# Two transformer blocks on one core: the wait for a stored table moved later, loads and norms at both ends reordered, queries computed over 258 columns

## The chip, the core and the metric

The kernel runs on one core of a Trainium2 chip. The metric is the device time of one execution, in microseconds (us). The engines have these names in profiles: PE is TensorE (matmuls; PEld its weight loads), DVE is VectorE, ACT is ScalarE, POOL is GpSimd, and SP is SyncE, which here only issues DMAs. A q behind a name (SPq) is the engine's own instruction queue.

## The reference, cut to what matters

A sequence of 256 tokens with 16 learned meta tokens ahead of it (L = 272 positions, D = 2048 features) goes through a first block; the 256 real tokens then go through a second one. All is float32.

```python
h = concat([meta, x])                                  # 272 positions
proj = rmsnorm(h, mix_norm_g) @ w_in                   # q, k, v of 8 + latents cq (512), ckv (256), k_pe (64)
out_a = neighbourhood_attention(q_a, k_a, v_a, rpb, meta_bias)   # 8 heads of 128, 4 x 64 grid
out_b = mla_attention(cq, ckv, k_pe, ...)              # 8 heads; q = rmsnorm(cq) @ w_q_up, k and v from ckv
h = h + concat([rmsnorm(out_a), rmsnorm(out_b)]) @ w_out
h = h + conv_glu(rmsnorm(h), ...)                      # width-3 convolution over positions
h = h[:, 16:]
# second block
proj = rms_norm(h, norm_mix) @ w_in_2
ya = moba_attention(q, k, v, rel_table)                # softmax(q k / sqrt(d) + rel_table[bucket(distance)])
yb = multiscale_pool(u, ...); yc = stick_breaking_attention(...)
h = h + (gates * branches(ya, yb, yc)) @ w_out_2
h = h + swiglu(rms_norm(h, norm_ffn))
out = rms_norm(h, norm_final)
```

## The kernel before, in words

Everything is stored transposed: features on the 128 partitions, positions along the free axis. `h` is 16 blocks of 128 x 272. A float32 product is made of three matmuls in a rounded type (fp32r): each operand is split in a high part and the rest (`xh`, `xl` for activations, `whi`, `wlo` for weights), and PE adds hi x hi, hi x lo and lo x hi (lines 1166 to 1168).

**The weight stream.** All weights come as 930 or so chunks of 128 x 1024 (512 KB), in the order of use, into four buffers `raw` (SP, line 307). ACT rounds a chunk (`high_part`, `whi`, line 414), DVE subtracts (`low_part`, `wlo`, line 718), and PE uses it. Both run two chunks ahead of PE (`AHEAD`). A new load goes out when DVE has made the low half of the buffer's chunk. A chunk is 24 matmuls of 128x128 weights (four output blocks `ob`, two contraction tiles, three products). A group is a run of chunks that fills the four banks of `acc`, which DVE empties. Every engine's program is written out in a fixed order; what another engine must have done is waited for by counting semaphores.

**The start.** SP issues the gains (`vec`), then in turn chunk and quarter of `h` (lines 310 to 313). ACT rounds chunks 0 and 1, then for each quarter of `h`: four `xh` blocks, the squares of the quarter, two chunks. DVE: low parts of chunks 0 and 1, then for each quarter four `xl` blocks, adding the squares into `ss`, `x_ready`, two low parts. PE starts on a pair of chunks when `x_ready` has counted a quarter. The norm's factor is applied when `acc` is emptied (`times_rms`).

**The first block's stages.** CQ (8 chunks) makes the query latent, CKV (8) the key latent, QUP (6) the queries of the latent attention (MLA), KVUP (4) its keys and values. Then QKV: 6 groups of 8 chunks make q, k, v of the neighbourhood attention (NA), 4 heads at a time, and between the chunks the eight MLA heads are computed, six chunks to a head (steps 0 to 5), NA heads 0 to 3 beside MLA heads 4 to 7. The other NA heads run beside the OUTB groups.

**The stored distances.** For the second block's attention a table of 8 heads x 512 distances is made just before QKV (PE line 1256, DVE line 905), in `dist`, which lies in the buffer `quad_a`. POOL writes it to DRAM 128 times over by one DMA of 2 MB (line 337), whose outermost dimension is the 8 heads. `quad_a` is also where NA's scores go (`sx_na`). DVE waits for the stored copy (`dist_stored`) ahead of the whole QKV loop. On POOL's queue the NA mask and the NA bias follow behind that DMA (lines 341 to 361); NA's first scores (step 2 of MLA head 4) need the bias.

**The end.** The last projection (DOWN2, 4 groups of 22 chunks) adds to `h`; after each group ACT squares four blocks (line 438) and DVE adds them to `ss`. Then one matmul with ones sums over partitions (line 1183), ACT takes Ln and Exp (lines 423, 425), DVE multiplies each of the 16 blocks by gain and factor (line 1142), and SP stores four quarters (line 324).

## Time and profile before

| | |
|---|---|
| median of 3 runs | 2908.0 us (2906.98 to 2910.27) |
| profiled execution | 2907.43 us, of which the span of its instructions 2905.7 us |
| PE busy | 2810.6 us, 97% of the span |
| DVE busy | 1654.5 us, 57% |
| ACT busy | 1244.4 us, 43% |
| POOL busy | 114.9 us, 4% |
| DMA | 499.99 MB, mean 172 GB/s |
| chain that ended last | PE 91%; DVE 3%; ACT 2%; DMA 2% |

PE's busy time counts modelled ends of pipelined matmuls; the distance between the starts of matmuls is the better measure of what one costs. The chain that ended last is followed back from the last instruction to what released each step; a share in it is time that shortening would give back, as long as nothing else is just behind. All times within the execution count from the start of its span.

### The profile page before, as it was taken

The page shows a single profiled execution, that of the slowest core. Times are in us where ns is not written, and L with a number is a line of the kernel's source. Part 1 is how long each engine was busy: PE and PEld are TensorE (multiplying, and loading weights), DVE is VectorE, ACT ScalarE, POOL GpSimd, SP SyncE. Part 2 cuts the span into 40 slices and gives each one's busy share as a digit, 9 for nine tenths or more (in the row PEclk, how much of TensorE's full clock was granted, in tenths as well). Part 3 has the DMA queues.
Part 4 walks back from the last instruction along what each step waited for, and adds up shares of the span by engine and source line. Part 5 has one row for each costly group of instructions (what it writes and reads, how often), then busy time and mean ns, then how long its engine had stood idle before and what let it go on. Part 6 is the DMA issues. An engine that isn't in the chain of part 4 may idle for free.

```text
span 2905.7 us, 58853 instructions
## 1 busy us (share of the span) xinstructions
PE 2810.6 (97%) x22990; PEld 2767.5 (95%) x22990; DVE 1654.5 (57%) x2128; ACT 1244.4 (43%) x1512; POOL 114.9 (4%) x133
## 2 busy tenths in 40 slices
PE   7589999999999999999999999999999999999997
PEld 7578899999999999999999999999999999999997
DVE  6255678666666654455555766555655555555444
ACT  5135555344343443443444555444443444334333
POOL 0001230000000000000000500000000000000000
PEclk9799999999999999999999999999999999999999
DMA  6433354555555554555555445555555555555545
GB/s 207 92 118 113 109 133 147 192 189 176 193 173 188 186 189 170 184 183 180 181 175 175 153 166 182 182 183 177 188 181 182 175 195 187 186 181 188 188 161 174
DMA packets 141133, 499.99 MB, mean 172 GB/s; under 512 B 17405, under 2 KB 19837, under 8 KB 141024
## 3 DMA queue, kind: packets, MB, share of 16 engines
q1 hardware_dynamic: 136912, 491.36, 49.8%
q0 software_dynamic: 4112, 7.02, 1.7%
q8 instruction: 87, 1.43, 0.2%
q14 instruction: 22, 0.18, 0.0%
HBM read 494.06 MB, written 4.19 MB: 171 GB/s over the span
## 4 chain that ended last, share of the span: by engine, by line
PE 91%; DVE 3%; ACT 2%; DMA 2%; issue 1%; DVEq 1%; ACTq 0%; SPq 0%
PE acc L1166 29%; PE acc L1168 28%; PE acc L1167 28%; DMA distances<-quads 2%; DVE wlo L718 1%; PE aux L1208 1%; ACT whi L414 1%; PE aux L1199 1%; PE aux L1271 0%; PE aux L1273 0%; PE aux L1265 0%; ACT quads L438 0%; DVE h L760 0%; DVE ss L745 0%; PE aux L1383 0%
## 5 line engine op out<-in xcount | busy, mean ns | idle before, releaser
L718 DVE TENSOR_TENSOR wlo<-raw,whi 128x1024 fp32r<-128x1024 f32 x926 | 1121.7, 1230 | 894.6 <-ACT whi L414 844.8
L1166 PE MATMUL acc<-xh,whi 128*128 128x256 f32 (+2 forms) x4976 | 1418.3, 285 | 63.3 <-DVE wlo L718 44.5
L1168 PE MATMUL acc<-xh,wlo 128*128 128x256 f32 (+2 forms) x4976 | 1404.4, 282 | 0.0
L1167 PE MATMUL acc<-xl,whi 128*128 128x256 f32 (+2 forms) x4976 | 1401.6, 282 | 0.0
L414 ACT ACTIVATE whi<-raw 128x1024 fp32r<-128x1024 f32 x926 | 954.5, 1054 | 858.1 <-PE acc L1168 813.3
L1166 PEld LDWEIGHTS acc<-xh,whi 128*128 128x128 f32 x4976 | 941.0, 189 | 74.2 <-DVE wlo L718 47.7
L1167 PEld LDWEIGHTS acc<-xl,whi 128*128 128x128 f32 x4976 | 938.6, 189 | 0.7
L1168 PEld LDWEIGHTS acc<-xh,wlo 128*128 128x128 f32 x4976 | 938.5, 189 | 0.0
L1166 PE MATMUL acc<-acth,whi 128*128 128x256 f32 x1408 | 398.0, 283 | 6.3 <-issue 6.3
L1167 PE MATMUL acc<-actl,whi 128*128 128x256 f32 x1408 | 397.5, 282 | 0.0
L1168 PE MATMUL acc<-acth,wlo 128*128 128x256 f32 x1408 | 397.3, 282 | 0.0
L1166 PEld LDWEIGHTS acc<-acth,whi 128*128 128x128 f32 x1408 | 267.3, 190 | 7.0 <-issue 6.7
L1167 PEld LDWEIGHTS acc<-actl,whi 128*128 128x128 f32 x1408 | 267.4, 190 | 0.0
L1168 PEld LDWEIGHTS acc<-acth,wlo 128*128 128x128 f32 x1408 | 267.3, 190 | 0.0
L738 DVE TENSOR_TENSOR quads<-acc,rstd 128x256 f32<-128x256 f32 (+2 forms) x140 | 59.0, 425 | 66.1 <-PE acc L1168 63.9
L1166 PE MATMUL acc<-mh,whi 128*128 128x256 f32 x256 | 72.3, 283 | 0.0
L1167 PE MATMUL acc<-ml,whi 128*128 128x256 f32 x256 | 71.9, 281 | 0.0
L1168 PE MATMUL acc<-mh,wlo 128*128 128x256 f32 x256 | 71.9, 281 | 0.0
L611 ACT ACTIVATE acth<-quads 128x1024 f32 (+1 forms) x22 | 23.3, 1060 | 113.0 <-DVE quads L1025 113.0
L608 ACT ACTIVATE quads<-quads 128x1024 f32<-128x1024 f32 x22 | 23.3, 1060 | 108.8 <-DVE quads L1011 56.3
L370 POOL DMA_DIRECT2D bias<-distances x16 | 8.7, 541 | 1113.0 <-PE acc L1168 829.6
L1025 DVE TENSOR_TENSOR quads<-acc,quads 128x256 f32<-128x256 f32 x88 | 37.4, 424 | 20.3 <-PE acc L1168 20.2
(272 smaller groups left out, 2360.8 us busy)
## 6 DMA issues: line engine op xcount, KB each, us to landing
raw<-in_wts SPq DMA_DIRECT2D x928, 512.0 KB, 4.2
h<-in_hT SPq DMA_DIRECT2D x4, 544.0 KB, 8.4
distances<-quads POOLq DMA_DIRECT2D x1, 2048.0 KB, 44.9
bias<-distances POOLq DMA_DIRECT2D x16, 128.0 KB, 2.4
out_T<-h SPq DMA_DIRECT2D x4, 512.0 KB, 2.9
bias<-in_rp POOLq DMA_DIRECT2D x16, 64.0 KB, 4.8
bias<-in_rp POOLq DMA_DIRECT2D x8, 44.0 KB, 4.4
bias<-in_rp POOLq DMA_DIRECT2D x8, 42.0 KB, 4.3
```

Source lines behind the costliest of these rows:

```text
L370: pool.dma_start(bias2[:, t, :], bass.AP(dist_dram.tensor, i * (DISTS + 1) + (SEQ - 1 - t * P), [[HEADS * (DISTS + 1) - 1, P], [1, SEQ]])) ...
L414: act.activation(whi[:, slot_of(at, j), :], raw[:, slot_of(at, j), :], ACT.Copy).then_inc(hi_ready, 1)
L608: act.activation(quad_b[:, :, 0:SEQ], quad_b[:, :, 0:SEQ], ACT.Silu).then_inc(silu_out, 1)
L611: act.activation(acth[:, bass.ds(i * 4, 4), :], quad_a[:, :, 0:SEQ], ACT.Copy).then_inc(act_hi, 1)
L718: dve.tensor_tensor(wlo[:, slot_of(at, j), :], raw[:, slot_of(at, j), :], whi[:, slot_of(at, j), :].bitcast(F32), ALU.subtract).then_inc(l ...
L738: dve.tensor_tensor(dst(ob), acc[0:rows, ob, 0:n], scale[0:rows, cols], ALU.mult)\
L1025: dve.tensor_tensor(quad_a[:, ob, 0:SEQ], acc[:, ob, 0:SEQ], quad_b[:, ob, 0:SEQ], ALU.mult)\
L1166: pe.matmul(dst, hi, x_hi(kt), start=kt == 0, stop=False)
L1167: pe.matmul(dst, hi, x_lo(kt), start=False, stop=False)
L1168: last = pe.matmul(dst, lo, x_hi(kt), start=False, stop=kt == chunks * per_chunk - 1)
L1199: last = pe.transpose(aux[0:nk, kt, t * a.rows:(t + 1) * a.rows], a.sx[0:a.rows, t, k:k + nk], ident_s[0:a.rows, 0:a.rows])
L1208: last = pe.matmul(aux[:, 3, 0:a.nq], a.vt[0:nk, kt, :], a.pt[0:nk, kt, 0:a.nq], start=kt == 0, stop=kt == len(a.kt) - 1)
```

## The change

Four things are done.

1. DVE's wait for `dist_stored` moves from ahead of the QKV loop to just ahead of the first NA scores (step 2, `na == 0`).
2. Queries are computed only for the 258 positions from `Q0` = 14 on (`xtail`): in CQ, in the two QUP groups and the two rope groups, and in the q groups of QKV. The unused 14 columns of `qnope`, `qrope` and the q part of `qkv` are set to zero at the start.
3. At the start SP issues the first quarter of `h` ahead of the first chunk, and waits for quarter 0 before it issues chunk 1 and for quarter 1 before it issues quarter 2. ACT and DVE do the first quarter of `xh` and `xl` before the first two chunks. `x_ready` now counts every two blocks of `xl`, before the squares, and PE waits for it chunk by chunk; the squares have a count of their own (`sq_used`). Later waits on `x_ready` are shifted by 4.
4. At the end the final gain is multiplied into `h` by ACT (`times_final_g`), block by block after the squares of each of the first three groups and after Exp for the last; the last four blocks are squared one by one and summed over partitions by PE, without DVE's additions; DVE multiplies a whole quarter by the factor in one instruction. ACT's and DVE's loops over the groups of DOWN2 are written out.

```diff
             sp.dma_start(vec[:], vecs).then_inc(vec_landed, 16)
-            for q in range(4):
-                load(q, q)
+            def load_h(q):
                 sp.dma_start(h[:, 4 * q:4 * q + 4, :], hT[:, 4 * q:4 * q + 4, :]).then_inc(h_landed[q], 16)
+
+            load_h(0)
+            load(0, 0)
+            sp.wait_ge(h_landed[0], 16)
+            load(1, 1)
+            load_h(1)
+            load(2, 2)
+            sp.wait_ge(h_landed[1], 16)
+            load_h(2)
+            load(3, 3)
+            load_h(3)
...
-            high_parts(At(-AHEAD, 0), AHEAD)
             for q in range(4):
                 act.wait_ge(h_landed[q], 16)
-                if q:
-                    act.wait_ge(x_ready, q)
                 for b in range(4 * q, 4 * q + 4):
                     act.activation(xh[:, b, :], h[:, b, :], ACT.Copy, scale=vec[:, VEC["mix_g"] + b:VEC["mix_g"] + b + 1])\
                         .then_inc(xh_ready, 1)
+                if q == 0:
+                    high_part(At(-AHEAD, 0), 0)
+                    high_part(At(-AHEAD, 0), 1)
+                else:
+                    act.wait_ge(sq_used, q)
                 act.activation(quad_b[:, :, :], h[:, 4 * q:4 * q + 4, :], ACT.Square).then_inc(sq_ready, 1)
...
+            def times_final_g(b):
+                act.activation(h[:, b, META:L], h[:, b, META:L], ACT.Copy,
+                               scale=vec[:, VEC["final_g"] + b:VEC["final_g"] + b + 1]).then_inc(hg_ready, 1)
+
+            for k in range(3):
+                residual(AT_DOWN2.past(k * CF, k), 4 * k, None, slice(META, L), None, CF)
+                act.drain()
+                for b in range(4 * k, 4 * k + 4):
+                    times_final_g(b)
+            at = AT_DOWN2.past(3 * CF, 3)
+            high_parts(at, CF)
+            act.wait_ge(x_ready, 23)
+            for ob in range(4):
+                act.wait_ge(bank_free, groups_behind(at, 4, 4 + ob + 1))
+                act.activation(quad_b[:, ob, 0:SEQ], h[:, DB - 4 + ob, META:L], ACT.Square).then_inc(sq_ready, 1)
+            inv_rms(rstd[:, META:L], aux[:, 3, META:L], D, ss_sum, 7, rs_ready)
+            for b in range(DB - 4, DB):
+                times_final_g(b)
...
-            low_parts(At(-AHEAD, 0), AHEAD)
             dve.wait_ge(vec_landed, 16)
             for q in range(4):
...
+                    if b % 2:
+                        last.then_inc(x_ready, 1)
+                if q == 0:
+                    low_part(At(-AHEAD, 0), 0)
+                    low_part(At(-AHEAD, 0), 1)
                 dve.wait_ge(sq_ready, q + 1)
-                add_squares(L).then_inc(x_ready, 1)
+                add_squares(L).then_inc(sq_used, 1)
...
             dve.memset(ss_na[:], 0.0)
-            dve.wait_ge(dist_stored, 16)
             for j in range(6 * CD):
...
                 elif step == 2:
+                    if na == 0:
+                        dve.wait_ge(dist_stored, 16)
                     if na >= 0:
                         scaled_scores(NA, na, bias, (bias_masked, na + 1))
...
             dve.wait_ge(rs_ready, 7)
-            for b in range(DB):
-                last = dve.scalar_tensor_tensor(h[:, b, META:L], h[:, b, META:L],
-                                                vec[:, VEC["final_g"] + b:VEC["final_g"] + b + 1], rstd[:, META:L],
-                                                ALU.mult, ALU.mult)
-                if b % 4 == 3:
-                    last.then_inc(out_ready, 1)
+            for q in range(4):
+                dve.wait_ge(hg_ready, 4 * q + 4)
+                hq = h[:, 4 * q:4 * q + 4, META:L]
+                dve.tensor_tensor(hq, hq, rstd[:, META:L].unsqueeze(1).to_broadcast([P, 4, SEQ]), ALU.mult)\
+                    .then_inc(out_ready, 1)
...
             for j in range(CD):
-                if j % 2 == 0:
-                    pe.wait_ge(x_ready, j // 2 + 1)
-                chunk(AT_CQ, j, CD, x1(xh), x1(xl), L)
+                pe.wait_ge(x_ready, j + 1)
+                chunk(AT_CQ, j, CD, xtail(xh), xtail(xl), NQ)
...
-            group(AT_QUP, 2, x1(lath), x1(latl), L)
+            group(AT_QUP, 2, xtail(lath), xtail(latl), NQ)
...
             for j in range(6 * CD):
-                chunk(AT_QKV.past(j // CD * CD, j // CD), j % CD, CD, x1(xh), x1(xl), L)
+                if j // CD % 3 == 0:
+                    chunk(AT_QKV.past(j // CD * CD, j // CD), j % CD, CD, xtail(xh), xtail(xl), NQ)
+                else:
+                    chunk(AT_QKV.past(j // CD * CD, j // CD), j % CD, CD, x1(xh), x1(xl), L)
...
-            token_sums(x_ready, 20)
+            pe.wait_ge(x_ready, 23)
+            pe.matmul(aux[:, 3, META:L], ones_s[:], ss[:, META:L], start=True, stop=False)
+            for ob in range(4):
+                pe.wait_ge(sq_ready, 20 + ob)
+                last = pe.matmul(aux[:, 3, META:L], ones_s[:], quad_b[:, ob, 0:SEQ], start=False, stop=ob == 3)
+            last.then_inc(ss_sum, 1)
```

DVE's order where the QKV loop begins, before: `wlo` is the low part of a weight chunk, `rs_a` is cleared to hold NA's sums, `aux` holds MLA head 0's rotated queries.

```order
L905 TENSOR_TENSOR quads<-aux,neg_s 8x512 [waits dist_sum]
L907 MEMSET rs_a 128x272
L718 TENSOR_TENSOR wlo<-raw,whi 128x1024 [waits hi_ready,dist_stored]
L816 TENSOR_TENSOR sqr<-aux,tab 64x272 [waits mla_sums]
L817 TENSOR_TENSOR qg<-qg,tab 64x272
L718 TENSOR_TENSOR wlo<-raw,whi 128x1024 [waits hi_ready]
```

The same place and the place of the first NA scores, in the changed kernel (about 100 DVE instructions lie between the two):

```order
L939 TENSOR_TENSOR quads<-aux,neg_s 8x512 [waits dist_sum]
L941 MEMSET rs_a 128x272
L744 TENSOR_TENSOR wlo<-raw,whi 128x1024 [waits hi_ready]
L842 TENSOR_TENSOR sqr<-aux,tab 64x272 [waits mla_sums]
...
L855 TENSOR_TENSOR kr<-tab,sq_60 64x272
L857 TENSOR_TENSOR qr<-sqr,sq_60 64x258
L812 SCALAR_TENSOR_TENSOR quads<-aux,bias 86x816 [waits bias_masked,na_scores,dist_stored]
L815 TENSOR_REDUCE quads<-quads 86x3
```

The wait has left the low part of a chunk and now stands on the instruction that already waits for the NA bias.

SP's order at the start, as the difference between the two programs (+ is the changed kernel; `raw` is a weight chunk):

```order
 L310 DMA vec<-in_vecs 128x292
+L312 DMA h<-in_hT 128x1088
 L307 DMA raw<-in_wts 128x1024
-L313 DMA h<-in_hT 128x1088
+L307 DMA raw<-in_wts 128x1024 [waits h_landed0]
+L312 DMA h<-in_hT 128x1088
 L307 DMA raw<-in_wts 128x1024
-L313 DMA h<-in_hT 128x1088
+L312 DMA h<-in_hT 128x1088 [waits h_landed1]
 L307 DMA raw<-in_wts 128x1024
```

Quarter 0 of `h` now goes first, and chunk 1 and quarter 2 each wait for a landed quarter.

DVE's order at the end, before and then in the changed kernel (`h<-acc,h` empties the last group; `ss` holds the summed squares):

```order
L745 TENSOR_TENSOR ss<-ss,quads 128x256 [waits sq_ready]
L745 TENSOR_TENSOR ss<-ss,quads 128x256 x3
L1136 REGISTER_ALU
L1136 COMPARE_AND_BRANCH
L1142 SCALAR_TENSOR_TENSOR h<-h,vec,rstd 128x256 [waits rs_ready]
L1142 SCALAR_TENSOR_TENSOR h<-h,vec,rstd 128x256 x15
```

```order
L744 TENSOR_TENSOR wlo<-raw,whi 128x1024 [waits hi_ready] x22
L786 TENSOR_TENSOR h<-acc,h 128x256 [waits block_done] x3
L786 TENSOR_TENSOR h<-acc,h 128x256 [waits chunk_used]
L1178 TENSOR_TENSOR h<-h,rstd 128x4x256 [waits hg_ready,rs_ready]
L1178 TENSOR_TENSOR h<-h,rstd 128x4x256 [waits hg_ready] x3
```

The four additions of squares are gone from behind the last group, and sixteen instructions have become four.

## Rows read from the trace of the kernel before

**Rows 1.** The page: the chain that ended last, by line.

```profile
PE acc L1166 29%; PE acc L1168 28%; PE acc L1167 28%; DMA distances<-quads 2%; DVE wlo L718 1%; PE aux L1208 1%; ACT whi L414 1%; PE aux L1199 1%; PE aux L1271 0%; PE aux L1273 0%; PE aux L1265 0%; ACT quads L438 0%; DVE h L760 0%; DVE ss L745 0%; PE aux L1383 0%
```

**Rows 2.** Waits, 105 to 152 us: who for whom, total, times, longest us.

```profile
DVE wlo L718 <- DMA distances<-quads: 45.0, 1, 45.0
```

**Rows 3.** Windows: us, busy PE, PEld, DVE, ACT, POOL; PEclk; DMA share; GB/s.

```profile
113.40:151.20 37.80, 0.00 (x0) 0.00 (x0) 1.19 (x2) 1.53 (x2) 0.00 (x0) 0.53 0.46 51
151.30:156.80 5.50, 5.50 (x24) 5.50 (x25) 4.92 (x9) 0.00 (x0) 4.92 (x7) 0.50 0.76 204
```

**Rows 4.** Timeline of PE: start us, us, line, out<-in [idle before <-releaser].

```profile
107.07 1.08 PE L1262 MATMUL aux<-sq,ones_s 128*128 128x272 f32 x4
...
110.35 0.29 PE L1167 MATMUL acc<-xl,whi 128*128 128x272 f32 x1
...
113.10 0.29 PE L1168 MATMUL acc<-xh,wlo 128*128 128x272 f32 x1
151.29 0.59 PE L1166 MATMUL acc<-xh,whi 128*128 128x272 f32 x1 [37.89 <-DVE wlo L718]
...
156.86 1.31 PE L1271 MATMUL aux<-kn,qn 128*86 128x272 f32 x5
...
202.25 0.85 PE L1262 MATMUL aux<-sq,ones_s 128*128 128x272 f32 x3
...
211.70 1.15 PE L1271 MATMUL aux<-kn,qn 128*86 128x272 f32 x4
```

**Rows 5.** DMA queues, 112 to 150 us: packets, MB, share of 16 engines.

```profile
q0 software_dynamic: 477, 1.97, 47.6%
```

**Rows 6.** The page: the weight queue over the whole span, in the same columns.

```profile
q1 hardware_dynamic: 136912, 491.36, 49.8%
```

**Rows 7.** DMA issues, 203 to 204 us: one weight load, KB, us to landing.

```profile
raw<-in_wts SPq DMA_DIRECT2D x1, 512.0 KB, 3.3
```

**Rows 8.** Timeline of ACT, 199 to 218 us.

```profile
200.79 1.05 ACT L414 ACTIVATE whi<-raw 128x1024 fp32r<-128x1024 f32 x1
...
217.57 1.05 ACT L414 ACTIVATE whi<-raw 128x1024 fp32r<-128x1024 f32 x1
```

**Rows 9.** Timeline of POOL and DVE: the first bias masked, the first NA scores.

```profile
160.75 1.94 POOL L361 TENSOR_TENSOR bias<-bias,mask_s 86x816 f32<-86x816 f32 x1 [3.95 <-DMA bias<-in_rp]
...
265.97 0.99 DVE L786 SCALAR_TENSOR_TENSOR quads<-aux,bias 86x816 f32<-86x816 f32 x1
```

**Rows 10.** DMA issues, one at 1.32 us and one at 1.79 us.

```profile
raw<-in_wts SPq DMA_DIRECT2D x1, 512.0 KB, 4.0
...
h<-in_hT SPq DMA_DIRECT2D x1, 544.0 KB, 5.3
```

**Rows 11.** Timeline of ACT, DVE and PE at the start.

```profile
9.94 1.74 ACT L498 ACTIVATE xh<-h,vec 128x272 fp32r<-128x272 f32 x4
...
12.86 2.00 DVE L745 TENSOR_TENSOR ss<-ss,quads 128x272 f32<-128x272 f32 x4
...
14.91 0.60 PE L1166 MATMUL acc<-xh,whi 128*128 128x272 f32 x1 [14.91 <-DVE ss L745]
```

**Rows 12.** Timeline of ACT, 545 to 575 us (chunks of 258 columns; five steps).

```profile
557.13 1.06 ACT L414 ACTIVATE whi<-raw 128x1024 fp32r<-128x1024 f32 x1 [1.83 <-PE acc L1168]
...
571.56 1.06 ACT L414 ACTIVATE whi<-raw 128x1024 fp32r<-128x1024 f32 x1 [1.82 <-PE acc L1168]
```

**Rows 13.** Timeline of PE and DVE at the end.

```profile
2893.96 0.98 PE L1183 MATMUL aux<-ss,ones_s 128*128 128x272 f32 x2 [3.81 <-DVE ss L745]
...
2896.00 6.42 DVE L1142 SCALAR_TENSOR_TENSOR h<-h,vec,rstd 128x256 f32<-128x256 f32 x16 [2.09 <-ACT rstd L425]
```

**Rows 14.** Groups by line and form, DVE: busy us, mean ns | idle before.

```profile
L1020 DVE TENSOR_TENSOR quads<-quads,rstd 128x1024 f32<-128x1024 f32 x11 | 13.4, 1218 | 0.0
```

**Rows 15.** DMA queues, 2896 to 2906 us.

```profile
q1 hardware_dynamic: 2112, 2.10, 61.3%
```

**Rows 16.** Timeline of DVE between the first two DOWN2 groups.

```profile
2702.38 4.62 DVE L718 TENSOR_TENSOR wlo<-raw,whi 128x1024 fp32r<-128x1024 f32 x4
```

More of the change, by code:

```diff
@@ L232, in build @@
         xh_ready = sem("xh_ready")
-        sq_ready = sem("sq_ready")
+        sq_ready, sq_used = sem("sq_ready"), sem("sq_used")
         x_ready = sem("x_ready")
@@ L503, in _, with latent @@
             inv_rms(rstd[:], aux[:, 3, 0:L], D, ss_sum, 1, rs_ready)
-            def latent(at, k0, blocks, gain):
+            def latent(at, k0, blocks, gain, c0):
                 act.wait_ge(bank_free, groups_behind(at, 4, 4 + 4))
                 for k in range(blocks):
-                    act.activation(lath[:, k0 + k, :], quad_a[:, k, :], ACT.Copy, scale=vec[:, gain + k:gain + k + 1])
-                return act.activation(quad_b[:, 0:blocks, :], quad_a[:, 0:blocks, :], ACT.Square)
-            latent(AT_CQ, 0, CQB, VEC["cq_g"]).then_inc(lat_hi, 1)
+                    act.activation(lath[:, k0 + k, c0:L], quad_a[:, k, c0:L], ACT.Copy,
+                                   scale=vec[:, gain + k:gain + k + 1])
+                return act.activation(quad_b[:, 0:blocks, c0:L], quad_a[:, 0:blocks, c0:L], ACT.Square)
+            latent(AT_CQ, 0, CQB, VEC["cq_g"], Q0).then_inc(lat_hi, 1)
             high_parts(AT_CKV, 4)
-            inv_rms(rs_a[:], aux[:, 3, 0:L], CQB * P, lat_sum, 1, lat_rs)
+            inv_rms(rs_a[:, Q0:L], aux[:, 3, Q0:L], CQB * P, lat_sum, 1, lat_rs)
             for j in range(4, CD):
                 high_part(AT_CKV, j)
-            latent(AT_CKV, CQB, CKVB, VEC["ckv_g"])
+            latent(AT_CKV, CQB, CKVB, VEC["ckv_g"], 0)
             act.activation(kpe_g, kpe, ACT.Copy, scale=vec[0:ROPE, VEC["k_rope_g"]:VEC["k_rope_g"] + 1])
@@ L705, in _ @@
             act.preload_act_table_set(LN_EXP)
-            with act.Fori(0, 2) as i:
-                for k in range(2):
-                    residual(shifted(Turn(AT_DOWN2, i, 2 * CF, 2), k * CF, k), i * 8 + 4 * k, None, slice(META, L), None,
-                             CF)
-            inv_rms(rstd[:], aux[:, 3, 0:L], D, ss_sum, 7, rs_ready)
+            def times_final_g(b):
[15 more added lines that the diff above has]
+                times_final_g(b)
         @block.vector
@@ L843, in _ @@
             dve.memset(ss[:], 0.0)
+            for q in (qnope[:, :, 0:Q0], qrope[:, :, 0:Q0], qkv[:, 0:HEADS, 0:Q0]):
+                dve.memset(q, 0.0)
             dve.drain()
@@ L915, in evict_group @@
                         half, part = divmod(j // CD, 3)
+                        c0 = 0 if part else Q0
                         times_rms(AT_QKV.past(j - CD + 1, j // CD), CD,
-                                  lambda ob: qkv[:, part * HEADS + 4 * half + ob, :], slice(0, L))
+                                  lambda ob: qkv[:, part * HEADS + 4 * half + ob, c0:L], slice(c0, L))
                 if step == 0:
@@ L1238, in _ @@
                     for k in range(CQB):
-                        last = pe.matmul(aux[:, 3, 0:L], ones_s[:], quad_b[:, k, :], start=k == 0, stop=k == CQB - 1)
+                        last = pe.matmul(aux[:, 3, Q0:L], ones_s[:], quad_b[:, k, Q0:L], start=k == 0, stop=k == CQB - 1)
                     last.then_inc(lat_sum, 1)
             pe.wait_ge(lat_ready, 1)
-            group(AT_QUP, 2, x1(lath), x1(latl), L)
-            group(AT_QUP.past(2, 1), 2, x1(lath), x1(latl), L)
+            group(AT_QUP, 2, xtail(lath), xtail(latl), NQ)
+            group(AT_QUP.past(2, 1), 2, xtail(lath), xtail(latl), NQ)
             for g in range(2):
-                group(AT_QUP.past(4 + g, 2 + g), 1, x1(lath), x1(latl), L, width=ROPE, row=4 * ROPE, per_chunk=4)
+                group(AT_QUP.past(4 + g, 2 + g), 1, xtail(lath), xtail(latl), NQ, width=ROPE, row=4 * ROPE, per_chunk=4)
             pe.wait_ge(lat_hi, 2)
```

34 lines of the change are left out of this document (18 added, 16 removed).

## The prediction

> **What bounds the kernel now.** I read the chain that ended last first. It is PE almost throughout: the three product lines make 85% of it [rows 1]. So a change pays if it takes columns from PE or idle time from in front of it. One entry is not an engine: the store of the distances is 2% of the chain, some 45 us. The waits of the stretch from 105 to 152 us show where it sits: DVE's low part of a weight chunk waits 45.0 us for that DMA [rows 2], and behind this instruction PE stands idle 37.89 us [rows 4]. The windows show the rest: PE's clock is at its lower level of 1.2 GHz for the 5.50 us that follow the idle time (PEclk 0.50) [rows 3]. At the ends the trace shows two more stretches in which PE is not at work: PE starts at 14.91 us [rows 11], and behind the last product come 3.81 us of idle time, one matmul and a tail from 2896.00 us on [rows 13].
>
> **Part 1, the wait.** What it costs is read from PE's timeline, by the same piece of program with and without it. In MLA head 0 the square sums start at 107.07 us and the first scores at 156.86, 49.8 us later; in head 2, which like head 0 has no group to empty there, it is 202.25 to 211.70, 9.45 us [rows 4]. The difference, 40.3 us, holds the idle time and the slow clock behind it. What is late next at that place is what is late in head 2, so it is in the 9.45 already. The wait itself lands on DVE's first NA scores. Behind them on DVE stand all the low parts of weights, and PE would wait for these; but before the change the first NA scores come at 265.97 us [rows 9], and the transfer had landed at 150 (105 + 45.0). Moved up by 40, they still come some 75 us after it. The bias stands behind the transfer on POOL's queue: it was masked at 162.7 us [rows 9], and nothing of that moves as long as the transfer takes its 45 us, which leaves over 60 us too (265.97 - 40.3 - 162.7).
>
> What is new is that weight loads now run beside the transfer; the trace has no such stretch. The transfer alone keeps 47.6% of 16 DMA engines busy at 477 packets in 38 us [rows 5]. If it is spread over all 16, the loads have 52% left and need about 35% in this stage, and nothing is lost. If it sits on the 8 engines of its outermost dimension, these are 95% busy, with 60 packets each in 38 us, 0.64 us a packet. A weight row of 4 KB costs 2905.7 x 16 x 0.498 / 136912 = 0.17 us of an engine [rows 6]. A load is 8 such rows per engine; taken in turn with the transfer's packets it takes 8 x (0.64 + 0.17) = 6.5 us, where the stage uses a load every (202.25 - 107.07 - 40.3) / 12 = 4.6 us [rows 4]. So each falls back 1.9 us, some 13 us over the 7 loads that fit in 45 us. Against it stands slack: a load goes out when the low half behind the high part of 200.79 us is made, at 203.2, lands 3.3 us later [rows 7] and is used at 217.57 [rows 8], 11 us to spare; and PE itself is two chunks behind ACT. What could leak through are scores and exponentials that ACT does behind a late chunk. Ends: 0 and 8 us; I take 1.5, near the free end, because the spare 11 us swallows most of 13. Part 1: -40.3 + 1.5.
>
> The Trainium skill ("DMA: Bandwidth & Descriptors", Rules for kernel authors) says that an access pattern whose slowest dimension is below 16 confines a DMA to at most that many engines, here 8. That speaks for the second case; 47.6% of 16 fits 8 busy engines, though it doesn't prove it.
>
> **Part 2, 258 columns.** From 110.35 to 113.10 us lie 22 starts of 272-column matmuls: 125 ns each [rows 4]. Chunks of 258 columns follow at (571.56 - 557.13) / 5 = 2.886 us, 120.2 ns a matmul [rows 12]. So 5 ns each. Affected are 8 chunks of 24 in CQ (192), 96 + 96 in QUP, 384 in QKV's q groups. QUP and QKV: 576 x 5 = 2.9 us; CQ is in part 3. Ends: 1.5, if the waits on DVE in each head eat the half, and 3.2. DVE's and ACT's shorter instructions between CQ and CKV, about a dozen on the path, give 14 columns or some 15 ns each: 0.2 us. The three small memsets are before any data has landed.
>
> A rule of the skill ("TensorE: Matmul & The Clock Gate", Back-to-back issue gap) has the spacing set by weight load and matmul together. Were the weight load alone the limit, 14 columns would buy nothing; the two spacings above differ, so the trace is against that.
>
> **Part 3, the start.** Loads land almost in the order of issue: the first at 1.32 + 4.0 = 5.3 us, the second at 1.79 + 5.3 = 7.1 [rows 10]. Now the quarter of h is first, so it is there at about 5.4, the chunk at 7.1. ACT: `xh` 5.5 to 7.2 (1.74 for four [rows 11]), high part 0 (1.05 [rows 8]) to 8.25. DVE: `xl` to 7.9, low part 0 (1.2, the last of 4.62 us for four [rows 16]) to 9.5. PE starts at 9.5 where it started at 14.91: 5.4 us. SP's new waits set what comes next: chunk 1 goes out at 5.5 and lands at 8.7, quarter 1 at 10.1, chunk 2 at 11.5, chunk 3 only after quarter 1, at 14.7. ACT does high part 3 ahead of the second quarter: to 15.8, then `xh`; DVE low part 3 to 17.0, two `xl` blocks to 17.9. PE, on its slow clock first (24 took 5.50 us with 272 columns [rows 3], so some 5.2), ends chunk 0 at 14.7, chunk 1 at 17.6, and waits 0.3. From there each pair of chunks takes PE 5.8 us and DVE 1.65 + 1.9 (squares, from 2.00 [rows 11]) + 2.3 = 5.8, a tie. `x_ready` no longer waits for the squares, which is why PE can run at all at this pace. At CQ's end the gain is then 5.4, plus 192 x 5 ns = 1.0, less 0.3 and 0.1: 6.0 us. Ends: 3, if chunk 3 or the clock's rise is 3 us later, and 7.
>
> **Part 4, the end.** The last product ends at 2893.96 - 3.81 = 2890.15 us. Emptying the bank takes to 2890.7, one Square block 0.44 (a quarter of 1.74 [rows 11]) to 2891.2, one matmul of half of 0.98 [rows 13], since the other sums are already in the bank, to 2891.7; Ln and Exp take as now 2896.00 - 2894.94 = 1.06, to 2892.8. DVE starts 3.2 us earlier. Its four instructions take 1.22 us each [rows 14] against 6.42 for sixteen [rows 13]; ACT's last four gains (1.74) end before the fourth. The stores are then the limit: their packets take 61.3% of 10 us, 6.1 us on 16 engines [rows 15], close to the 6.42. So of the 1.5 us that DVE saves, only the earlier first store (1.3 instead of 1.6) and the closed gaps (0.3 to 0.6) count: 0.8. Part 4: 4.0 us; ends 3.0 and 4.7.
>
> In the three earlier groups ACT has the four gains (1.74, with a drain 1.8) between the squares and the next high part, the one for the group's chunk 2. PE wants that chunk two chunks after the last product, 5.7 us. Before: emptying 0.6, squares 1.05, DVE's additions 2.0 [rows 11], low part 1.2 [rows 16]: 4.9. Now ACT's side is the longer one: 0.6 + 1.05 + 1.8 + 1.05 (high part) + 1.2 = 5.7, and waits between engines of 0.2 make 5.9. PE stands 0.2 us, at two of the boundaries: 0.4; ends 0 and 0.8.
>
> **Sum.** -40.3 + 1.5 - 2.9 - 0.2 - 6.0 - 4.0 + 0.4 = -51.5 us. The profiled execution took 2907.4, so 2855.9; the median of the runs is 0.6 higher: 2856.5 us.
>
> **The rivals.**
> - Weights late beside the transfer. For it: 95% busy engines, if they are 8. Against: 11 us of slack. Full price 8 instead of 1.5: 2863. The skill's rule on engines (above) makes this the rival it names. Chance 0.13.
> - The start gives back its gain: SP, blocked on quarter 0 and 1, leaves the DMA engines idle, chunk 3 and then `xl` come 3 us later: 2859.5. For it: two round trips of about 5 us are now in series. Against: the stores of work ACT and DVE have meanwhile. Chance 0.10.
> - Columns buy nothing (the skill's weight-load rule): 2.9 and 1.0 lost, 2860.4. The measured spacings are against it: 0.02.
> - The change doesn't do what it says: the 45 us come back at the first NA scores or the bias. It would need the transfer to last 60 us longer; then the wait is the excess. 0.01.
> - Slower than before. The mechanism: on the shared engines the transfer goes first, and the loads land only when it ends. PE still has the four chunks whose weights were in at 105 us, four times 4.6 us from 113 on, so it stands from about 131. With the transfer's 45 us this costs 19 us and 3 for the slow clock, 2877, still faster. To be slower by 0.2%, 2913.8, PE must lose 57 us there, which asks for a transfer of 26 + 57 = 83 us, 1.85 times the one seen, with no load landing. For it: nobody has seen the two together. Against: queues of equal kinds shared the engines at the start, where every load landed. Chance 0.02, with 0.02 more for the 2877.
>
> **How the numbers follow.** The forecast has 0.70. Within it: start 3 to 7, columns 1.5 to 3.2, end 3.0 to 4.7, contention 0 to 4, and one period of slow clock more or fewer elsewhere, worth half of 5.5 us [rows 3]. Few of these go wrong together: 2850 to 2862. The range takes in the first two rivals and most of their sum: 2849 to 2866. What a measurement can tell from no change is 0.2%, 5.8 us. Only the slower rival and the return of the wait reach that side: faster 0.97, same 0.01, slower 0.02.
>
> **What would show it.** PE's idle time at 113 us gone, the clock at full level from about 15 us to the first DOWN group; the distances' time to landing between 45 and 60 us and the weight loads beside it at 3 to 8 us instead of 3.3; no wait on `dist_stored` in the list. First matmul at 9 to 10 us, CQ's end 6 us earlier. Chunks of q groups at 2.89 us. DVE's last stretch four instructions of 1.2 us, beginning some 3 us earlier behind the last product, and the span ending 11.5 us behind it instead of 15.6. The prediction is wrong if the raw loads land later than 14 us beside the transfer, if ACT waits for them there, or if PE waits for `xl` in CQ by more than 1 us in total.

## The result, and the profile after

The changed kernel takes 2871.6 us (median of 4 runs, 2868.3 to 2875.0), the kernel before beside it 2907.5 (2906.8 to 2910.3). The ratio is 0.9875, with a 95% interval of 0.9858 to 0.9892. The change gains 36 us, not 51, and ends 5.6 us above the range forecast. The profiled execution took 2870.8 us with a span of 2869.1.

The page's chain of the changed kernel, by line, answers [rows 1]; the row of the weight queue, q1, answers [rows 6]. In the rows below q0 is GpSimd's software queue and q10 ScalarE's hardware queue.

```profile
q1 hardware_dynamic: 136912, 491.36, 52.4%
...
PE acc L1199 29%; PE acc L1201 29%; PE acc L1200 29%; DVE wlo L744 1%; DMA raw<-in_wts 1%; ACT whi L424 1%; PE aux L1241 1%; PE aux L1232 0%; PE aux L1306 0%; PE aux L1308 0%; DMA h<-in_hT 0%; PE aux L1300 0%; DVE h L786 0%; PE aux L1421 0%
```

The store of the distances is gone from the chain, and 1% of `raw<-in_wts` is new: weight loads. The waits between 90 and 180 us (who for whom, total, times, longest) say how much, where [rows 2] had the one wait of 45.0.

```profile
POOL bias L358 <- issue: 47.7, 1, 47.7
DVE wlo L744 <- ACT whi L424: 30.1, 10, 8.3
ACT whi L424 <- DMA raw<-in_wts: 23.5, 6, 8.4
```

VectorE no longer waits for the store. (The first row is POOL's own: the neighbourhood attention's mask goes out just behind the store, at 101.74 us, and lands with it, 48.1 us later. The first bias is masked at 161.9 us and used at 234.3, so nobody waits for it.) ScalarE waits 23.5 us for weights, and VectorE's low parts wait behind it. The DMA issues at 97.4, 104.5, 113.2 and 117.7 us (KB, us to landing), and the store's own, answer [rows 7].

```profile
raw<-in_wts SPq DMA_DIRECT2D x1, 512.0 KB, 3.3
...
raw<-in_wts SPq DMA_DIRECT2D x1, 512.0 KB, 21.8
...
raw<-in_wts SPq DMA_DIRECT2D x1, 512.0 KB, 25.7
...
raw<-in_wts SPq DMA_DIRECT2D x1, 512.0 KB, 27.4
...
distances<-quads POOLq DMA_DIRECT2D x1, 2048.0 KB, 47.8
```

A load takes 3.3 us alone and up to 27.4 us beside the store. (A further load, issued at 109.9 us, takes 22.7.) ScalarE's timeline shows the rhythm in which they arrive, where [rows 8] had no wait.

```profile
126.39 1.06 ACT L424 ACTIVATE whi<-raw 128x1024 fp32r<-128x1024 f32 x1 [8.44 <-DMA raw<-in_wts]
132.64 1.06 ACT L424 ACTIVATE whi<-raw 128x1024 fp32r<-128x1024 f32 x1 [4.71 <-DMA raw<-in_wts]
138.90 1.06 ACT L424 ACTIVATE whi<-raw 128x1024 fp32r<-128x1024 f32 x1 [2.88 <-DMA raw<-in_wts]
145.18 1.06 ACT L424 ACTIVATE whi<-raw 128x1024 fp32r<-128x1024 f32 x1 [3.46 <-DMA raw<-in_wts]
```

The starts are 6.26 us apart: that is the 6.5 us for a load that takes turns with the store. New is the 8.44 us in front of the first. PE's longest waits here are one of 5.40 us, which ends at 147.98, and this one:

```profile
129.19 2.59 PE L1241 MATMUL aux<-pt,vt 91*128 91x258 f32 x6 [4.47 <-DVE pt L830]
```

In the windows (columns as in [rows 3]) the second and third are stretches at the lower clock; one begins right behind PE's wait, the other 1.4 us before its end.

```profile
100.00:148.00 48.00, 36.68 (x245) 31.61 (x243) 17.62 (x30) 17.63 (x35) 2.47 (x3) 0.95 0.61 117
129.50:132.90 3.40, 3.40 (x13) 2.94 (x12) 0.00 (x0) 0.26 (x1) 0.00 (x0) 0.50 0.78 165
146.60:153.40 6.80, 5.42 (x24) 5.45 (x25) 5.47 (x11) 2.12 (x2) 2.57 (x3) 0.50 0.51 193
```

The start and the end, from the timelines of PE, ScalarE and VectorE, answer [rows 11] and [rows 13].

```profile
10.22 0.55 PE L1199 MATMUL acc<-xh,whi 128*128 128x258 f32 x1 [10.22 <-DVE wlo L744]
...
19.51 0.39 PE L1199 MATMUL acc<-xh,whi 128*128 128x258 f32 x1 [1.84 <-DVE xl L881]
...
16.31 1.06 ACT L424 ACTIVATE whi<-raw 128x1024 fp32r<-128x1024 f32 x1 [2.77 <-DMA raw<-in_wts]
17.28 1.75 ACT L505 ACTIVATE xh<-h,vec 128x272 fp32r<-128x272 f32 x4
...
2856.64 0.28 PE L1201 MATMUL acc<-acth,wlo 128*128 128x256 f32 x1
2856.76 0.59 PE L1490 MATMUL aux<-ss,ones_s 128*128 128x256 f32 x2
2857.19 1.89 PE L1493 MATMUL aux<-quads,ones_s 128*128 128x256 f32 x8
...
2860.11 4.63 DVE L1178 TENSOR_TENSOR h<-h,rstd 128x1024 f32<-128x1024 f32 x4 [2.72 <-ACT rstd L435]
```

PE starts 4.7 us earlier, at 10.22 (4.2 us against the second trace of before, see experiment 1); the wait of 2.77 us for chunk 3 then makes `xh` late, and PE stands 1.84 us from 17.7 on. From the start of the last product to the span's end it is now 12.45 us, against 15.86 in the first trace of before and 16.15 in the second. All three signs by which the prediction called itself wrong are there: loads later than 14 us, ScalarE's waits for them, and PE's wait for `xl` of over 1 us.

### The profile page after: what moved, and what is told of

Same layout as the page of the kernel before. It is cut to its first block, busy times and chain, and to the rows that moved or that the text cites. A ratio compares the mean times of both kernels' runs of the same rounds, so it can differ in the third digit from the quotient of the medians.

```text
span 2869.1 us, 58709 instructions
## 1 busy us (share of the span) xinstructions
PE 2811.4 (98%) x22998; PEld 2767.3 (96%) x22998; DVE 1651.9 (58%) x2115; ACT 1251.6 (44%) x1531; POOL 114.2 (4%) x133
## 4 chain that ended last, share of the span: by engine, by line
PE 91%; DVE 3%; ACT 2%; DMA 1%; issue 1%; DVEq 1%; ACTq 0%; SPq 0%
PE acc L1199 29%; PE acc L1201 29%; PE acc L1200 29%; DVE wlo L744 1%; DMA raw<-in_wts 1%; ACT whi L424 1%; PE aux L1241 1%; PE aux L1232 0%; PE aux L1306 0%; PE aux L1308 0%; DMA h<-in_hT 0%; PE aux L1300 0%; DVE h L786 0%; PE aux L1421 0%; PE aux L1314 0%
## 5 line engine op out<-in xcount | busy, mean ns | idle before, releaser
L1199 PE MATMUL acc<-xh,whi 128*128 128x256 f32 (+2 forms) x4976 | 1419.1, 285 | 26.4 <-DVE wlo L744 16.7
L764 DVE TENSOR_TENSOR quads<-acc,rstd 128x256 f32<-128x256 f32 (+1 forms) x140 | 59.0, 425 | 65.1 <-PE acc L1201 64.3
## 6 DMA issues: line engine op xcount, KB each, us to landing
distances<-quads POOLq DMA_DIRECT2D x1, 2048.0 KB, 47.8
```

What stands on the lines that cost most here:

```text
L764: dve.tensor_tensor(dst(ob), acc[0:rows, ob, 0:n], scale[0:rows, cols], ALU.mult)\
L1199: pe.matmul(dst, hi, x_hi(kt), start=kt == 0, stop=False)
```

## The experiments

All ratios are against the kernel before, run beside them. The changed kernel itself was timed only with the result; differences from it are differences of medians from other rounds, in which the kernel before had medians of 2907.1 to 2908.8 us. So such a difference under some 2 us says nothing. "Lead" is how much earlier than in the kernel before VectorE makes the low part of the same weight chunk.

**1. The kernel before, once more.** Nothing is edited; it serves as a second trace. The expectation counts the traces read until then.

> The kernel before once more, unchanged, for a second trace of it on another chip. All eight traces of other kernels so far show the turn of 16 chunks in the second feed-forward network at 45.58 us, the one trace of the kernel before at 45.37 us, 2.1 us over its eleven turns. If the kernel sets it, this trace has 45.37 again. If the chip or the execution does, it has 45.58, and 2 us of the leads read against the old trace are no effect of the change.

Windows of the second feed-forward network in the first trace of before, the second, and the changed kernel:

```profile
2200.00:2600.00 400.00, 400.00 (x3386) 400.00 (x3385) 220.58 (x231) 162.65 (x160) 0.00 (x0) 1.00 0.54 184
```

```profile
2200.00:2600.00 400.00, 400.00 (x3371) 400.00 (x3370) 219.75 (x230) 162.46 (x159) 0.00 (x0) 1.00 0.55 183
```

```profile
2200.00:2600.00 400.00, 400.00 (x3371) 400.00 (x3369) 216.46 (x226) 160.70 (x157) 0.00 (x0) 1.00 0.56 186
```

In the same 400 us the first trace has 3386 matmuls, the other two 3371. From one turn of 16 chunks to the next it is 45.60 us in VectorE's low parts here, as in all traces but the first, which has 45.39 (the expectation has 45.58 and 45.37; the 0.21 between them is the same). So the kernel does not set it; the execution or the chip does. The second trace (2906.1 us, span 2904.5) also lacks the slow clock of the first at 1133 to 1140 us, so leads against the old trace were off by up to 4.6 us. All leads in the table below are read against the second.

**2. Only the wait moved**, in the kernel before. The line taken out stands ahead of the QKV loop, the new ones in step 2 of each head:

```diff
-            dve.wait_ge(dist_stored, 16)
...
+                    if na == 0:
+                        dve.wait_ge(dist_stored, 16)
```

> The kernel before with only VectorE's wait for the stored distances moved to the first neighbourhood scores; order of the loads, the norms at both ends and the columns as before. Theory A: the wait gives back only 25 to 27 us of its 40.3, as in the changed kernel: 2880 to 2883 us, and PE waits in the stage for late loads. Theory B1 (the stall comes from the earlier start, which puts loads and store in another phase): the wait gives its 39 to 40 us, 2867 to 2869 us. The turn of 16 chunks in the second feed-forward network takes 45.39 us as in the kernel before if PE's code position sets it (PE's instructions are those of before), 45.60 us if the other engines' do.

2881.9 us (2881.0 to 2883.0), ratio 0.9912 (0.9895 to 0.9928): 25.5 us gained. The load issued at 109.8 us and the one at 123.1, and ScalarE's waits for weights from 90 to 270 us:

```profile
raw<-in_wts SPq DMA_DIRECT2D x1, 512.0 KB, 21.8
...
raw<-in_wts SPq DMA_DIRECT2D x1, 512.0 KB, 27.4
```

```profile
ACT whi L414 <- DMA raw<-in_wts: 23.5, 6, 8.3
```

These are the changed kernel's numbers, so neither the new start nor the columns have a part in them: theory A holds, B1 falls.

**3. The store in 16 gated pieces**, in the changed kernel. The run without the store that the expectation names gave no time. Its theory B: VectorE and ScalarE hold the stage back by their order or by the clock, and the store only coincides. The two waits for the store count to 256 here.

```diff
-            pool.dma_start(dist_dram.rearrange("c h d -> h c d"), dist.unsqueeze(1).to_broadcast([HEADS, P, DISTS + 1]))\
-                .then_inc(dist_stored, 16)
+            for n in range(16):
+                pool.wait_ge(chunk_used, AT_QKV.n + n)
+                pool.dma_start(dist_dram[8 * n:8 * n + 8].rearrange("c h d -> h c d"),
+                               dist.unsqueeze(1).to_broadcast([HEADS, 8, DISTS + 1])).then_inc(dist_stored, 16)
```

> The changed kernel with the store issued as 16 DMAs of 8 copies, the n-th once PE has used n chunks of the QKV products. Same bytes, spread over some 45 us. Theory A (a load waits behind what the store has queued ahead of it on the shared engines): a piece holds those engines for 3 us, a load lands after at most 3.3 + 3 = 6.3 us where the ring of four chunks allows about 11 us, so nothing waits and the time is that of the kernel without the store, 2857 to 2860 us. Theory A' (the shared rate alone counts, however the store is cut): loads land after 16 to 27 us as now, 2869 to 2874 us. Theory B as for the run without the store: no change.

2857.3 us (2855.3 to 2859.1), ratio 0.9829 (0.9812 to 0.9845), 14.3 us below the changed kernel. The first load beside a piece (103.4 us) and the slowest of the stage, then the window that stands against 36.68 above:

```profile
raw<-in_wts SPq DMA_DIRECT2D x1, 512.0 KB, 4.9
...
raw<-in_wts SPq DMA_DIRECT2D x1, 512.0 KB, 5.6
```

```profile
100.00:148.00 48.00, 46.11 (x324) 40.26 (x323) 25.59 (x44) 21.14 (x42) 5.86 (x11) 1.00 0.62 140
```

The same bytes, and the missing 15 us are back: theory A holds, B falls. PE is busy 46.1 of 48 us, and the clock stays at full level. The gates also stretch the store: its pieces go out from 99.5 to 165.4 us, not in one go of 45 us. That its lower mean rate has a part in the gain is not excluded by this run alone; the rows of single loads, here and in experiments 6 and 7, show the hold itself.

**4. The store in two DMAs of 64 copies, back to back.**

> The changed kernel with the store as two DMAs of 64 copies, issued back to back. If both halves lie on the same eight engines, as theory A has it (the heads, the slowest dimension, set the engines, not the number of copies), the transfer takes 46 to 49 us in all and the time stays at 2869 to 2874 us. If the halves lie on different engines, the transfer is over in 24 to 30 us but meets all of a load's packets, and the time falls by 3 to 8 us, to 2864 to 2868 us.

2884.2 us (2881.1 to 2886.2), ratio 0.9922 (0.9905 to 0.9938): 13 us slower than the changed kernel, against both cases. The queues from 102 to 130 us, with the load issued at 105.6 and ScalarE's waits from 100 to 180:

```profile
q0 software_dynamic: 614, 1.44, 91.1%
```

```profile
raw<-in_wts SPq DMA_DIRECT2D x1, 512.0 KB, 38.2
```

```profile
ACT whi L425 <- DMA raw<-in_wts: 26.7, 2, 24.9
```

The halves do lie on different engines (91% of 16), but the store is not faster: its 4 KB packets take 1.1 us each instead of 0.6, and it has landed 48 us after its first issue, as in the changed kernel (47.8). And for 28 us (103.2 to 131.5) no packet of a load moved at all, though loads were issued.

**5. The store in 16 pieces without the gates**, all issued at once.

> The changed kernel with the store cut into 16 DMAs of 8 copies, all issued at once: the cut of the paced run without its gates. What the traces of the runs so far show: the store alone moves about 12.5 packets of 4 KB in a microsecond, on 8 engines at 0.6 us each or on 16 at 1.1 us each, and an engine serves some 22 to 26 of the store's packets before the first packet of a weight load gets its turn. Theory A (what lies queued on an engine counts, so the gates made the gain): the pieces fill all 16 engines, loads stand for 20 to 38 us, and the time is that of the store in two halves, 2878 to 2886 us. Rival (the size of one DMA counts, since a load gets its turn between two DMAs): loads land after 5 to 8 us and the time is that of the paced run, 2856 to 2860 us.

2874.8 us (2870.6 to 2877.9), ratio 0.9881 (0.9864 to 0.9897): between the two ranges, 3 us below A's, and from the changed kernel (2871.6) it can't be told. The loads issued at 105.1 and 113.8 us:

```profile
raw<-in_wts SPq DMA_DIRECT2D x1, 512.0 KB, 22.5
...
raw<-in_wts SPq DMA_DIRECT2D x1, 512.0 KB, 34.9
```

The loads are held as long as beside the whole store, so it is the gates and not the cut. Why it is 9 us better than the two halves stays open.

**6. The store in 4 pieces, gated every fifth chunk.**

> The changed kernel with the store as 4 DMAs of 32 copies, the n-th once PE has used 5 n chunks of the QKV products. A piece is 128 packets of 4 KB, 16 on each of 8 engines, 10 us. Theory A: a load issued just behind a piece stands for up to 10 us and lands after up to 13 us, about what the ring of four chunks covers (some 11 us), so PE waits 0 to 2 us for each of the four pieces: 2857 to 2866 us. Rival (a fixed hold of some 14 us at every DMA of the store, whatever its size): four holds, 2866 to 2880 us; the run in 16 pieces speaks against it already.

2857.9 us (2856.6 to 2859.1), ratio 0.9829 (0.9812 to 0.9845). The load issued at 146.7 us is the slowest; ScalarE's waits for weights, 95 to 260 us:

```profile
raw<-in_wts SPq DMA_DIRECT2D x1, 512.0 KB, 12.0
```

```profile
ACT whi L426 <- DMA raw<-in_wts: 0.9, 2, 0.7
```

The load lands 8.7 us late, and in all ScalarE waits 0.9 us: the slack of 11 us is real. The time is at the lower end of theory A's range, and the rival of a fixed hold falls.

**7. The store in 2 pieces, the second ten chunks later.** Ten chunks take PE some 46 us here, not 28: the second half went out at 151.6 us, 50.5 us behind the first.

> The changed kernel with the store as two DMAs of 64 copies, the second once PE has used 10 chunks of the QKV products, so 28 us behind the first: 32 packets of 4 KB on each of 8 engines, where the whole store has 64 and the quarter 16. Theory Q (an engine serves some 22 to 26 of the store's packets in a row, then takes turns): the first load behind each half lands after 15 to 20 us and the one behind it 6 us later; ScalarE waits 4 to 8 us for the first, and the time is 2860 to 2866 us. Rival T (they take turns from the first packet on and the late landings have another cause): loads land after 7 to 10 us and nothing waits, 2857 to 2860 us. Rival F (strictly first come, first served): the load behind the whole half lands after 20 to 24 us, two more at once behind it, 2862 to 2870 us.

2866.9 us (2865.6 to 2868.2), ratio 0.9861 (0.9846 to 0.9876), 0.9 us above theory Q's range. Loads issued at 105.0, 110.4 and 153.4 us:

```profile
raw<-in_wts SPq DMA_DIRECT2D x1, 512.0 KB, 20.6
...
raw<-in_wts SPq DMA_DIRECT2D x1, 512.0 KB, 16.4
...
raw<-in_wts SPq DMA_DIRECT2D x1, 512.0 KB, 21.8
```

Taking turns from the first packet (rival T) is refuted. Between "some 26 in a row" and "first come, first served" this run does not decide: the half has 32 packets an engine and ends soon after. By the forecasts F is the nearer one: the time lies in its range, and the first two loads land 1.2 us apart (125.6 and 126.8), not 6. The whole store decides against F, since its loads land 6.26 us apart while it still runs.

**8. The whole store from ScalarE's queue.** Its `dma_start` stands behind ScalarE's own wait for `dist_ready`.

> The changed kernel with the store issued by ScalarE's queue instead of GpSimd's, whole and at the same place; nothing else differs. The traces so far: the store's packets alone had an engine for some 26 in a row (17 us on 8 engines, 28 us on 16) before a weight load got its first packet there; after that the two took turns. Theory S (that run in a row belongs to GpSimd's software queue): from ScalarE's hardware queue the two take turns at once, the first load lands after 8 to 10 us and not 21.8, the waits of ScalarE for weights sink from 23.5 us to 5 to 10, and the time falls by 5 to 11 us, to 2861 to 2867 us. Rival H (any queue's DMA holds the engine so): loads land after 16 to 27 us as now, 2869 to 2874 us. A second rival: ScalarE's own time to issue the 2 MB store is long (over 2 us) and delays its squares; then up to 3 us come on top of either.

2865.8 us (2864.7 to 2868.0), ratio 0.9852 (0.9836 to 0.9867): 5.7 us gained, inside theory S's range, but not for the reason given. The queues from 101 to 119 us, the same of the changed kernel from 102 to 119, then the load at 105.4 and ScalarE's waits for weights, 100 to 180:

```profile
q10 hardware_dynamic: 412, 0.84, 43.2%
q1 hardware_dynamic: 216, 0.79, 13.1%
```

```profile
q0 software_dynamic: 754, 0.96, 50.2%
q1 hardware_dynamic: 216, 0.79, 16.1%
```

```profile
raw<-in_wts SPq DMA_DIRECT2D x1, 512.0 KB, 21.8
```

```profile
ACT whi L421 <- DMA raw<-in_wts: 13.5, 3, 8.6
```

Both rows of q1 hold 0.79 MB, 192 rows of 4 KB. That is half of each of three loads, most likely the half on the engines that the store leaves alone (the rows name no engine). So the hold is there from a hardware queue too, with a longest wait of 8.6 us, and theory S falls. The gain comes behind it: this queue's packets are 2 KB at 0.30 us, and the loads behind the first land 2.6 to 3.2 us apart, not 6.26, which is faster than the stage needs them (ScalarE waits 13.5 us for weights, not 23.5). The mask and the bias, no longer behind the store on GpSimd's queue, also move to an earlier time; what that does was not tested.

**9. The start without SP's two waits.**

```diff
-            sp.wait_ge(h_landed[0], 16)
...
-            sp.wait_ge(h_landed[1], 16)
```

> The changed kernel without the SP queue's two waits for a quarter of h among the first loads; the order of the loads stays. Theory S (those waits issue chunk 3 only at 11.6 us, ScalarE waits 2.8 us for it, PE then 2.1 us, and the clock falls once more for 1.7 us): chunk 3 lands about 2 us earlier and the time falls by 2 to 4 us, to 2867.5 to 2869.5 us; the first product stays at 10 to 11 us. Rival (the first loads are bound by the engines' rate, and the waits only put them in the order in which they are used): h's first quarter or chunk 0 lands later, the first product starts 1 us or more later, and the time stays within 1 us or grows by up to 3 us.

2871.4 us (2867.6 to 2875.0), ratio 0.9872 (0.9856 to 0.9889): no change in the time. PE's first product and ScalarE's wait for chunk 3:

```profile
11.04 0.55 PE L1197 MATMUL acc<-xh,whi 128*128 128x258 f32 x1 [11.04 <-DVE wlo L742]
```

```profile
15.40 1.06 ACT L422 ACTIVATE whi<-raw 128x1024 fp32r<-128x1024 f32 x1 [1.57 <-DMA raw<-in_wts]
```

Both theories are half right. The first product is 0.8 us later, chunk 3 0.9 us earlier, PE has no gap and no second slow period in the first group, and the lead is 2.3 us larger at the stage of QUP and 2.4 at the QKV stage. That lead is then lost in stretches of slow clock further on (6.8 us of it at 267, where the changed kernel has 3.4, and another 3.4 us at 1100).

**10. Only the columns**, in the kernel before.

> The kernel before with the queries' products alone over the 258 columns that are used (the first latent, the queries' up products, two groups of eight of the QKV stage), with the same for what ScalarE and VectorE do on them. Theory A: 3 us less for the products, 0.2 us for the other engines' and perhaps 1 us in the first group: 2903 to 2905 us. Rival (the weight loads bound the pace, so fewer columns buy nothing): 2907 to 2908 us. A third: VectorE's zero fills at the start delay the first split of weights by about 1 us and eat part of it: 2904 to 2906 us.

2902.9 us (2901.0 to 2906.5, 10 runs), ratio 0.9984 (0.9975 to 0.9994): 4.5 us, interval 1.7 to 7.3. The lead grows by 0.8 us over QUP and KVUP and by 2.3 over the QKV stage, with 1.0 and 1.9 forecast; CQ's products take 26.4 us from first to last, against 27.2 in experiment 2, whose start is the same: 0.8 for the 1.0 forecast. The columns are worth about what their spacing says; that they buy nothing is refuted.

**11. The old end in the paced run.** ScalarE's, VectorE's and PE's code behind the last feed-forward group is that of the kernel before.

> The paced run with the end of the kernel before: norm after the last residual in one piece, loops over pairs of groups, 16 final multiplications of VectorE with gain and norm. In the trace of the changed kernel the stretch from the last product to the end of the span was 3.4 us shorter than before (12.5 against 15.8). Theory: the new end is worth 3 to 4 us: 2860 to 2862 us, the span ending 15 to 16 us behind the last product. Rival (the unrolled groups cost at their borders what the shorter tail brings): 2857 to 2859 us.

2862.5 us (2858.4 to 2864.6), ratio 0.9837 (0.9823 to 0.9850): 5.3 us above the paced run and 0.5 above the theory's range. VectorE's last row, and a window of the NA stage:

```profile
2853.12 6.42 DVE L1167 SCALAR_TENSOR_TENSOR h<-h,vec,rstd 128x256 f32<-128x256 f32 x16 [2.38 <-ACT rstd L437]
```

```profile
256.00:266.30 10.30, 10.30 (x35) 7.64 (x34) 3.85 (x8) 3.47 (x12) 5.51 (x8) 0.50 0.59 131
```

From the last product to the end it is 16.14 us, against 12.45 in the paced run: 3.7 us. The rest of the difference lies in front of the last product, where this execution has 10.2 us of slow clock that the paced one lacks, which costs half of that. That stretch is no effect of the end, so the end's worth is the 3.7 us and not the 5.3.

**12. Both findings together**: the gated store and the start without SP's waits.

> The changed kernel with both findings in it: the store in 16 gated pieces, and the first loads without the SP queue's two waits. In the traces the gates brought the lead over the kernel before at the QKV stage's end from 31.5 to 46.5 us, and the missing waits the lead at its start from 4.5 to 6.8 us. If both hold together: 2.4 us less than the paced run, 2854 to 2856 us. Rival (what the start gains is given back in a period of slow clock after some later wait, as in the run without the two waits, whose time did not move): 2856 to 2859 us, the lead at the QKV stage's start still 6.8 us.

2856.6 us (2855.5 to 2858.1), ratio 0.9828 (0.9815 to 0.9842). It beats the kernel before and the changed one; the 0.7 us to the paced run can't be told from nothing. The rival is nearer: at the QKV stage's end it is 2.2 us ahead of the paced run, at the last product 0.4 behind, with one slow stretch more (2714.7 us).

## Why the prediction was wrong, step by step

Leads in us against the second trace of before; the forecast's terms are put together by stage (40.3 - 1.5 + 1.9 for the QKV stage). The sums are the differences of the spans.

| stage | forecast | changed kernel | store in 16 gated pieces |
|---|---|---|---|
| start, to the end of the first two latent groups | 6.2 | 2.6 | 3.6 |
| QUP and KVUP | 1.0 | 0.7 | 0.7 |
| QKV stage | 40.7 | 26.2 | 41.7 |
| from there to the last product | -0.4 | 2.2 | 1.1 |
| tail | 4.0 | 3.7 | 3.7 |
| sum | 51.5 | 35.4 | 50.9 |

- **The step that failed is the price of the contention**, +1.5 with ends 0 and 8. The price comes out at some 16 us: in the QKV stage 14.5 us are missing beyond the 1.5, and experiment 3 brings back 15.6 by pacing alone. All three of its inputs were right. The transfer sits on 8 engines, as the Trainium skill ("DMA: Bandwidth & Descriptors", Rules for kernel authors) has it and the half loads of experiment 8 bear out. A load in turn with it takes 6.26 us, where 6.5 were worked out. The slack of 11 us was right too (experiment 6). What was missing is the hold ahead of the first turn: the store has its engines alone for its first 17 us or so, and some 14 of them stand in front of the first load (an estimate: its 21.8 us less 6.3 for its own turns and 1.1 until its first packet). With it the sum comes out. The first load is 21.8 - 3.3 = 18.5 us late; less 11, that is 7.5 (8.44 seen). Three more loads at 6.26 - 4.6 add 5. The 10.2 us at the lower clock cost 5 more, so 18 in all, of which some runs side by side. PE's own windows say the same: its busy time from 100 to 148 us is 9.4 us less than in the paced run, and with the clock's 5.1 that makes 14.5. The prediction had a reason against it: at the start every load landed. But there all loads are on one queue and wait for each other; no store of another queue was beside them.
- **The rival "weights late" was the right mechanism at half its size** (8 us, 2863); its price took in the turns and not the hold. The rival of the transfer going first, 2877 at 0.02, had the hold for all 45 us. The truth lies between them, and nothing in the trace of before excluded it: the first load's wait had no row. The ends of that term should have reached to the 22 us worked out for that rival.
- **The wait itself** is right. It moved to where it costs nothing (the first NA scores now come at 234.3 us, the store lands at 148.4), and with the contention gone the stage gains 41.7 us, where the forecast without its 1.5 has 42.2.
- **The start** was 3.6 us too good. PE began at 10.2, not 9.5; ScalarE waited 2.77 us for chunk 3 and PE 1.84 us for `xl`, not 0.3; the clock fell once more behind it. Taking out SP's waits gives back 2.3 us of the lead at that place (experiment 9 against the changed kernel) and 2.1 (experiment 12 against 3). But executions with the same start differ too: with the waits in, this lead is 1.5 to 3.8 us over eight traces. So the rival of the start, with a chance of 0.10, came true in good part; the rest is chance or open.
- **The columns and the end** are right: 1.9 + 1.0 + 1.0 forecast for columns, 2.3 + 0.8 + 0.8 seen in experiment 10; 4.0 for the end, 3.7 seen (3.4 against the first trace of before). The end's working was wrong in one point: PE makes all four sums of squares only behind its last product, since they stand there in its order, not one. On columns that buy nothing the prediction speaks of a weight-load rule; what the Trainium skill ("TensorE: Matmul & The Clock Gate", Back-to-back issue gap) states is that both together set the spacing. The 125 against 120.2 ns of the trace of before agree with it.
- **The borders of the DOWN2 groups** took 0.3 us each at the first and the third, so 0.6 where 0.4 was forecast. Between the QKV stage and the last product the changed kernel still gains 2.2 us where 0.4 of loss was forecast; no run shows why.
- **The clock** was not at full level from 15 us on: ahead of the DOWN2 groups it fell at 20, 129, 147 and 269 us, each time at a wait of 1.8 to 5.4 us of PE. A wait is not enough: PE also waits 2.4 us at 1098 and the clock stays. Each stretch of 3.4 us costs 1.7. This fits how executions of one kernel differ: without SP's waits one took 2867.6 us at a mean clock of 0.996, another 2875.0 at 0.993. The paced run's trace has one such stretch before the tail, the changed kernel's five.

What stays open: what ends the hold, how much of the paced run's gain is its lower mean rate, and why the cut into 16 without gates does better than the cut into two.

## What to carry to other kernels

When a bulk transfer is freed from the path, ask what it does to the latency of small transfers that now run beside it, not only to their rate: a slack that covers each load's share did not cover the hold ahead of the first. Cut such a transfer into pieces shorter than the slack and gate each on the consumer's progress. Cutting into 16 without gates gave nothing (2874.8 for 2871.6 us), and two halves on all 16 engines cost 13 us. And before a few us are read out of two traces, take the old kernel's trace twice.

## What the runs showed of the hardware

- An engine that has begun on a large DMA of one queue served about 0.1 MB of it before the first packet of another queue: at least 0.83 MB on 8 engines by 119 us in the changed kernel (q0's row has 0.96, of which 0.12 are the mask), 0.84 MB on 8 by then from ScalarE's queue, and 1.44 MB on 16 by 130 us for the two halves. That is 103, 105 and 90 KB an engine, as lower bounds; the first load packets beyond the free engines' half come 1 to 3 us later. Only then did the queues take turns (loads 6.26 us apart in the changed kernel).
- The store from 8 partitions to memory moved some 50 GB/s whether on 8 engines (0.6 us for 4 KB), on 16 (1.1 us), or in 2 KB packets (0.30 us). So the number of engines does not bound it, and the engines are taken all the same; what does bound it is not shown.
- Of 14 traces of this family, 13 have the turn of the same loop at 45.60 us and one at 45.39, and the kernel before is in both groups.
